# A two-layer attention and retention trunk on one core: another order of work at the opening, between the layers and at the end, and the rotation of the attention's q and k made by VectorE alone

## The chip, the cores and the metric

The kernel runs on one core of one Trainium2 chip. A core has TensorE (PE: matmuls, and transposes made as matmuls), VectorE (DVE), ScalarE (ACT), GpSimd (POOL) and SyncE (SP, which here only issues DMAs). PE writes to PSUM, a memory of eight banks; the other tiles lie in SBUF. The metric is the device time in microseconds (us) of one execution, lower is better. The engines run their own instruction streams and meet only at semaphores, on which an instruction waits until a count is reached.

## The reference, cut to what matters

```python
for layer in range(2):
    h = rms_norm(x, norm_g[layer])                     # x: 1024 rows of 1024
    qa, ka, va, ga, qr, kr, vr, gr, gm = split(h @ w_in[layer])
    qa = rope(rms_norm(qa per head, attn_q_norm))      # 8 heads of 64
    ka = rope(rms_norm(ka per head, attn_k_norm))      # 2 kv heads of 64
    ya = (silu(ga) * softmax(qa ka' / 8) va) @ w_branch_attn[layer]
    yb = (silu(gr) * group_norm(retention(rope(qr), rope(kr), vr))) @ w_branch_ret[layer]
    gates = sigmoid(gm)
    x = x + (gates[0] * ya + gates[1] * yb) @ w_out[layer]
out = rms_norm(x, final_norm_g)

# rope on one head, per axis, with x1, x2 the halves of the axis:
# [x1 * c - x2 * s,  x1 * s + x2 * c]
```

All is float32. A product of float32 matrices is made of three matmuls of two-part numbers (hi and lo, where lo is the number less its rounded hi part): hi·hi, hi·lo and lo·hi. So each operand of a product has a hi tile and a lo tile, which some engine has to make.

## The kernel before, in words

x stays in SBUF (xh, 8 tiles of 128 rows, T = 8). A layer has these stages.

*Projection and preparation for attention, once for each of two groups of heads (j = 0, 1).* For j = 0 a row tile t is normed by VectorE into one of two buffers hb (`norm_x`, L1287; it needs the squares' sums that ScalarE makes at L967, and VectorE's `mean_square`, a chain of twelve tiny instructions), turned by PE (`turn_x`, L591), copied as hi part by ScalarE (`hi_x`, L989), and its lo part made by VectorE (`lo_x`, L1343). Then PE projects q (4 heads), k and v of the tile (`project`, L566 to L568, 24 matmuls of 384 columns). ScalarE squares and copies the result (L1002 to L1004), VectorE sums the squares and frees the bank (`outputs`, L1354, L1357). In three batches VectorE makes the inverse roots (`norms`). Then each tile's q and k, 5 heads of 64 = 320 columns, are normed and rotated (`rotate`, L1380 on): VectorE multiplies by the root and the gain (L1385, L1388) and, with the halves exchanged, by the sines (L1396, two instructions of 160 columns); GpSimd multiplies by the cosines (L420) and adds the two (L425). ScalarE takes the hi parts, VectorE the lo parts (`split`, L1404, L1406), PE turns them (`turn`, L663), and ScalarE and VectorE keep what was turned (L1023, `keep_k` L1412). In the code PE has at the end four gate projections between the turns, each in two parts.

*Attention of the group:* 32 tiles of scores, softmax and values; here PE is kept busy.

*Retention, gates and branches*, which the change does not touch but for the layer number in the semaphores' counts.

*The output product.* The matrix product with w_out is made by a scheme of 7 products of halved matrices (N_P = 7) instead of 8. Product p takes a left operand (a half of xm, or a sum of two, `left_sum`, L1689) and a right one (a block of w_out, or a sum, L537). ScalarE makes their hi parts (L1200, L1218), VectorE the left lo parts (`left_lo`, L1698), GpSimd the right sums and the right lo parts (L544). PE makes product p of 48 matmuls into four banks (L938 to L940), and VectorE adds them to one or two quarters of x (`add_up`, L1711; four banks, one or two instructions of 512 columns each). Two sets of four banks take turns, so product p + 2 waits for `add_up(p)`. A product loops over k outside and the four row tiles i inside, so all four results are complete only at its end.

*Order.* Each engine's order is written out by hand, in the code of its block. The layers are a hardware loop (`Fori(0, DEPTH)`) on every engine, and at the loop's head the engines wait on `phase_end` until PE, ScalarE and VectorE have all drained. At the opening ScalarE issues all constants and waits for them before it issues x; GpSimd makes the hi and lo parts of the first weights (L383, L389); VectorE makes the retention's decay factors (L1298 to L1329) before the loop is entered. At the end of a layer VectorE's order is `add_up(4)`, `add_up(5)`, `mean_square`, two `norm_x`, `add_up(6)`; the last layer's end then norms rows 2 to 7 in place (L1747) and two queues write the rows to `out`.

## Time and profile before

| what | value |
|---|---|
| median of 3 runs | 1934.1 us (1932.88 to 1935.05) |
| the profiled execution's own time | 1931.47 us |
| its span, first to last instruction | 1929.7 us |
| PE busy | 1812.3 us (94%) |
| VectorE busy | 1061.7 us (55%) |
| GpSimd busy | 836.7 us (43%) |
| ScalarE busy | 668.2 us (35%) |
| chain that ended last: PE, VectorE, issue, DMA | 69%, 16%, 6%, 3% |

An engine's busy share is an average over stages with different limits. The chain that ended last is followed back from the last instruction, at each step to what released it. In timelines a row is a start, a duration, the engine, the line, what was written and read, and in brackets how long the engine had been idle before it and who released it. PEclk is the clock granted to TensorE, 1.00 being its full 2.4 GHz and 0.50 the lower level of 1.2 GHz.

### The profile page before, as it was taken

To read this page: it belongs to the slowest core of one execution; us is meant where nothing else is said; L and a number is where in the kernel's file an instruction comes from. 1 tells how busy PE (TensorE), PEld (TensorE's weight loads), DVE (VectorE), ACT (ScalarE), POOL (GpSimd) and SP (SyncE) were. 2 spreads that over 40 slices of the span, in tenths; PEclk is the share of its full clock that TensorE was granted. 3 is DMA by queue.
4 is the path that set the end of the run, shared out by engine and by line. 5 is a ranking of instruction groups with operands and counts; after the bars stand their busy time and mean duration, and the time that the engine had idled before them with its cause. 6 is when DMAs were issued, how large, how long until landed. Compare 5 with 4: busy or idle time off the path is not lost.

```text
span 1929.7 us, 32806 instructions
## 1 busy us (share of the span) xinstructions
PE 1812.3 (94%) x10784; PEld 1590.6 (82%) x10784; DVE 1061.7 (55%) x2246; ACT 668.2 (35%) x1564; POOL 836.7 (43%) x652
## 2 busy tenths in 40 slices
PE   3899989999999999999878998999999999999995
PEld 3788978899999888888667887789999988888874
DVE  6979678635554210107977987794444541110478
ACT  4368438622212100003433872683222210000133
POOL 3348337623422323335823773485223422323383
PEclk9999999999999999999989999999999999999998
DMA  7100000101111111124130001001011111112132
GB/s 248 33 12 13 27 23 23 45 23 44 35 30 34 44 55 44 44 65 164 34 124 23 23 1 49 9 15 45 24 43 43 44 33 44 44 54 65 50 136 88
DMA packets 129593, 96.40 MB, mean 50 GB/s; under 512 B 15664, under 2 KB 114224, under 8 KB 129456
## 3 DMA queue, kind: packets, MB, share of 16 engines
q1 hardware_dynamic: 125920, 84.56, 14.1%
q10 hardware_dynamic: 3536, 10.17, 1.5%
q8 instruction: 66, 1.08, 0.2%
q14 instruction: 71, 0.58, 0.1%
HBM read 82.13 MB, written 12.58 MB: 49 GB/s over the span
## 4 chain that ended last, share of the span: by engine, by line
PE 69%; DVE 16%; issue 6%; DMA 3%; ACT 2%; POOL 2%; DVEq 1%; SPq 1%; ACTq 0%; POOLq 0%
PE ps L566 17%; PE ps L568 17%; PE ps L567 17%; PE ps L701 5%; PE ps L690 4%; DVE xh L1711 3%; PE ps L714 2%; PE ps L716 2%; DMA xh<-xs 2%; PE ps L807 2%; DVE pT_lo L1477 1%; PE ps L791 1%; DVE zqk L1388 1%; DVE rtb L1396 1%; DVE hT_lo L1698 1%
## 5 line engine op out<-in xcount | busy, mean ns | idle before, releaser
L566 PE MATMUL ps<-w_hi,hT_hi 128*128 128x256 f32 (+1 forms) x1280 | 390.3, 305 | 13.9 <-DVE hT_lo L1343 9.3
L568 PE MATMUL ps<-w_hi,hT_lo 128*128 128x256 f32 (+1 forms) x1280 | 376.5, 294 | 0.0
L567 PE MATMUL ps<-w_lo,hT_hi 128*128 128x256 f32 (+1 forms) x1280 | 376.3, 294 | 0.0
L383 POOL TENSOR_SCALAR w_hi<-raw 128x1024 fp32r<-128x1024 f32 x100 | 108.4, 1084 | 398.5 <-PE ps L568 368.4
L566 PEld LDWEIGHTS ps<-w_hi,hT_hi 128*128 128x128 f32 x1280 | 245.0, 191 | 17.4 <-issue 12.5
L566 PE MATMUL ps<-hT_hi,w_hi 128*128 128x512 f32 x640 | 254.6, 398 | 0.0
L567 PE MATMUL ps<-hT_lo,w_hi 128*128 128x512 f32 x640 | 251.1, 392 | 0.0
L568 PE MATMUL ps<-hT_hi,w_lo 128*128 128x512 f32 x640 | 250.8, 392 | 0.0
L567 PEld LDWEIGHTS ps<-w_lo,hT_hi 128*128 128x128 f32 x1280 | 245.2, 192 | 0.3
L568 PEld LDWEIGHTS ps<-w_hi,hT_lo 128*128 128x128 f32 x1280 | 244.6, 191 | 0.0
L389 POOL TENSOR_TENSOR w_lo<-raw,w_hi 128x1024 fp32r<-128x1024 f32 x84 | 207.5, 2470 | 6.0
L435 POOL TENSOR_SCALAR pp<-pp,rrc 128x1024 f32<-128x1024 f32 x128 | 144.4, 1128 | 109.0 <-DVE rrc L1482 102.1
L1667 DVE SCALAR_TENSOR_TENSOR tA<-tA,ps 128x512 f32<-128x512 f32 x32 | 21.8, 686 | 306.9 <-PE ps L568 306.9
L1477 DVE TENSOR_TENSOR pT_lo<-ps,pT_hi 128x512 fp32r<-128x512 f32 x256 | 164.3, 683 | 24.5 <-ACT pT_hi L1072 23.2
L482 POOL TENSOR_TENSOR ra<-ra,rb 128x256 f32<-128x256 f32 x64 | 47.7, 746 | 271.9 <-DVE rb L1532 271.9
L1469 DVE TENSOR_REDUCE nmx<-ps 128x1 f32<-128x1024 f32 x128 | 155.4, 1214 | 2.8 <-PE ps L690 2.8
L701 PE MATMUL ps<-idf,pp 128*128 128x128 f32 x1024 | 146.5, 279 | 10.5 <-DVE pT_lo L1477 8.1
L701 PEld LDWEIGHTS ps<-idf,pp 128*128 128x128 f32 x1024 | 111.2, 140 | 49.6 <-DVE pT_lo L1477 49.0
L1061 ACT ACTIVATE pp<-ps,nmx 128x1024 f32<-128x1024 f32 x128 | 144.2, 1127 | 17.7 <-DVE nmx L1469 16.2
L1072 ACT CAST pT_hi<-ps 128x512 fp32r<-128x512 f32 x256 | 138.5, 590 | 29.6 <-PE ps L701 26.9
L690 PE MATMUL ps<-k_st,q_st 128*128 128x512 f32 x512 | 148.6, 412 | 0.0
L568 PEld LDWEIGHTS ps<-hT_hi,w_lo 128*128 128x128 f32 x640 | 121.4, 190 | 26.0
(175 smaller groups left out, 3543.0 us busy)
## 6 DMA issues: line engine op xcount, KB each, us to landing
raw<-w_in SPq DMA_DIRECT2D x168, 256.0 KB, 3.2
xs<-xh SPq DMA_DIRECT2D x2, 4096.0 KB, 17.6
xh<-xs SPq DMA_DIRECT2D x8, 1024.0 KB, 13.9
xh<-x ACTq DMA_DIRECT2D x4, 1024.0 KB, 10.1
raw<-w_a SPq DMA_DIRECT2D x16, 256.0 KB, 2.9
raw<-w_r SPq DMA_DIRECT2D x16, 256.0 KB, 3.2
w<-w_o SPq DMA_DIRECT2D x4, 1024.0 KB, 11.6
ctA<-rope_a SPq DMA_DIRECT2D x8, 256.0 KB, 2.9
```

Source lines behind the costliest of these rows:

```text
L383: nc.gpsimd.tensor_scalar(place(pos)[0], raw[:, slot], 1.0, 1.0, ALU.mult, ALU.mult).then_inc(w_rounded, 1)
L389: nc.gpsimd.tensor_tensor(lo, raw[:, slot], hi.bitcast(F32), ALU.subtract).then_inc(w_ready, 1)
L435: nc.gpsimd.tensor_scalar(pp[:, tile % 3], pp[:, tile % 3], rrc[:, tile % 4:tile % 4 + 1], 1.0, ALU.mult, ALU.mult).then_inc(p_norm, 1)
L566: nc.tensor.matmul(outp, ah, bh, start=(start and i == 0), stop=False)
L567: nc.tensor.matmul(outp, ah, bl, start=False, stop=False)
L568: last = nc.tensor.matmul(outp, al, bh, start=False, stop=(stop and i == len(pairs) - 1))
L690: last = nc.tensor.matmul(ps[:, 2 * (tile % 2) + n, :], q_st[:, hh, t * P:(t + 1) * P], k_st[:, c, n * 512:(n + 1) * 512], start=(c == 0), ...
L701: last = nc.tensor.transpose(ps[:, 4 + g % 2, kb * P:(kb + 1) * P], pp[:, tile % 3, (4 * half + kb) * P:(4 * half + kb + 1) * P], idf[:])
L1061: nc.scalar.activation(pp[:, tile % 3], ps[:, 2 * s:2 * s + 2].rearrange("p a b -> p (a b)"), ACT.Exp, bias=nmx[:, tile % 4:tile % 4 + 1], ...
L1072: nc.scalar.copy(pT_hi[:, e % 2, 4 * half:4 * half + 4, (tile % 2) * P:(tile % 2 + 1) * P], ps[:, 4 + half].rearrange("p (k c) -> p k c", ...
L1469: V.tensor_reduce(nmx[:, tile % 4:tile % 4 + 1], ps[:, 2 * s:2 * s + 2].rearrange("p a b -> p (a b)"), AXX, ALU.max, negate=True).then_inc ...
L1477: V.tensor_tensor(pT_lo[o], ps[:, 4 + half].rearrange("p (k c) -> p k c", c=P), pT_hi[o].bitcast(F32), ALU.subtract).then_inc(p_lo, 1)
```

## The change

It has three parts.

**The layer loop is written out** on all engines (`for L in range(DEPTH)`), with constant counts in most waits in place of registers, and the wait of all engines for all at the layer's head is gone.

**Opening, border and end have another order.** At the opening SP and ScalarE issue x tile 0 and the first weights at once, the constants behind them. ScalarE makes the first weights' hi parts and VectorE their lo parts. Squares are now taken a row tile at a time (`square_row`, 1024 columns), rows 2 to 7 of them behind `outputs(0)`, `outputs(1)` and `outputs(2)`; VectorE has four `mean_square`s in place of two, and the decay factors stand between its tiles 2 and 6. In the output product, products 3, 4 and 5 change places; the right lo parts go from GpSimd to VectorE, two left sums (for products 5 and 6) from VectorE to GpSimd; product 6 (`last_product`) loops over the row tiles outside, so that they are completed one after another; VectorE's `mean_square` and first norms stand ahead of `add_up(5)`. In layer 0 PE makes the first two `turn_x` of the next layer inside product 6. At the end rows 0 to 3 are normed ahead of `add_up(5)`, rows 4 to 7 in two pairs behind `add_up(6)`.

**VectorE makes the whole rotation** of the attention's q and k: the product with the cosines and the sum, 128x320 each, are its instructions, and GpSimd's two per tile are gone. GpSimd's filling of the gate weights then stands alone ahead of the attention.

```diff
-LEFT = (((1, 0, 1),), ((0, 0, 1), (0, 1, 1)), ((0, 0, 1), (1, 0, -1)), ((1, 0, 1), (1, 1, 1)),
...
-B_SUMMED = (0, 2, 4, 5, 6)
+B_SUMMED = (0, 2, 3, 4, 6)
@@ sync
-            with sp.Fori(0, DEPTH) as L:
+            sp.dma_start(xh[:, 0, 0:512], xt[:, 0, 0:512]).then_inc(x_in[0], 16)
...
+            for L in range(DEPTH):
...
-                            sp.wait_ge(phase_end, 3 + L * PH_L + j * 3)
+                            if j == 0:
+                                sp.wait_ge(o_done, L * (4 * N_P) + 4 * N_P)
+                            else:
+                                sp.wait_ge(phase_end, L * PH_L + j * 3)
@@ gpsimd
                 with pool.Fori(0, KVH) as j:
-                    for t in range(T):
-                        bt = L * (KVH * T) + j * T + t
-                        pool.wait_ge(b_norm, bt * 2 + 2)
-                        if t >= 2:
-                            pool.wait_ge(b_lo, bt * 2 - 2)
-                        nc.gpsimd.tensor_tensor(rta[:, t % 2]..., zqk[:, t]..., ctA[:, 0, t:t + 1]..., ALU.mult).then_inc(b_cos, 1)
-                        pool.wait_ge(b_cos, bt + 1)
-                        pool.wait_ge(b_sin, bt * 2 + 2)
-                        nc.gpsimd.tensor_tensor(rta[:, t % 2], rta[:, t % 2], rtb[:, t % 2], ALU.add).then_inc(b_rot, 1)
-                        if t == 3:
-
-                            pool.wait_ge(b_proj, L * (KVH * T) + j * T + T)
-                            fill(0, 0, L * PER[0] + j * 3 + 2, n0 + j * N_B + 4)
+                    pool.wait_ge(b_proj, L * (KVH * T) + j * T + T)
+                    fill(0, 0, L * PER[0] + j * 3 + 2, n0 + j * N_B + 4)
...
-                right_lo(0)
-                right_lo(1)
                 right_sum(2, 4)
-                right_lo(2)
-                right_lo(3)
-                right_sum(4, 6)
...
+                right_sum(3, 6)
+                right_sum(4, 8)
+                left_sum(5)
                 right_sum(6, 10)
-                right_lo(6)
+                left_sum(6)
@@ tensor
+                def last_product(p):
...
+                    for i in range(4):
+                        pe.wait_ge(o_post, base + POSTS[p - 2] + len(INTO[p - 2]) * (i + 1))
...
+                        if L + 1 < DEPTH and i >= 1 and i <= 2:
+                            pe.wait_ge(o_post, base + POSTS[p - 1] + len(INTO[p - 1]) * (2 * i))
+                            turn_x(i - 1, L + 1)
@@ scalar
+            square_row(0)
+            act.wait_ge(idf_in, 16)
+            nc.scalar.copy(idr[:], idf[:]).then_inc(pro_act, 1)
+            first_hi(0)
+            first_hi(1)
...
                         outputs(t)
+                        if j == 0 and L == 0:
+                            if t < 3:
+                                square_row(2 + 2 * t)
+                                square_row(3 + 2 * t)
@@ vector
+            def mean_square(a, b, squares, nw):
+
+                dve.wait_ge(a_sq, squares)
...
                         if t >= 2:
                             dve.wait_ge(b_rot, bt - 1)
+                            dve.wait_ge(b_lo, bt * 2 - 2)
+                        V.tensor_tensor(rta[:, t % 2].rearrange("p (h d) -> p h d", d=HD), z,
+                                        ctA[:, 0, t:t + 1].to_broadcast([P, GRP + 1, HD]), ALU.mult).then_inc(b_cos, 1)
...
+                        dve.wait_ge(b_cos, bt + 1)
+                        dve.wait_ge(b_sin, bt * 2 + 2)
+                        V.tensor_tensor(rta[:, t % 2], rta[:, t % 2], rtb[:, t % 2], ALU.add).then_inc(b_rot, 1)
...
+                            if L == 0 and t < 2:
+                                if t == 0:
+                                    mean_square(2, 4, 4, 24)
+                                norm_x(0, t + 2)
                             if t == 1:
-                                mean_square(L, 1)
-                            if t + 3 < T:
+                                mean_square(4, 8, SQ0(L + 1) if L == 0 else SQ0(L) + N_SQ, 36 if L == 0 else NW_0 + L * NW_L + 12)
+                            if t + 3 < T and (L or t):
                                 norm_x(L, t + 3)
+                        if j == 0 and L == 0:
+                            if t == 2:
+                                decays_start()
+                            if t == 4:
+                                decays_ratio()
+                            if t == 6:
+                                decays_end()
...
                 add_up(4)
-                add_up(5)
-                mean_square(L + 1, 0)
+
+                mean_square(0, 4, SQ0(L + 1) + 8, NW_0 + (L + 1) * NW_L)
...
+                else:
+                    for t in range(4):
+                        norm_out(t)
+                    add_up(5)
+                    add_up(6)
```

The first place is ScalarE's order at the opening. Before (junk and sqj are where squares go, xh is x, sq and zqk are the squares and the copy of a projected tile):

```order
L960 CAST idr<-idf 128x128
L962 ACTIVATE lgw<-lgw 128x16
L967 ACTIVATE junk,ss<-xh 128x512 x12
L977 ACTIVATE dec<-dec 128x8x6
L982 UNCONDITIONAL_BRANCH
```

And now, from the first copied tile on:

```order
L1023 ACTIVATE junk,ss<-xh 128x1024
L1041 CAST hT_hi<-ps 128x4x128 x2
L1055 ACTIVATE sq<-ps 128x320
L1056 COPY zqk<-ps 128x320
L1057 CAST v_st<-ps 128x64
L1023 ACTIVATE junk,ss<-xh 128x1024 x2
L1041 CAST hT_hi<-ps 128x4x128 x2
L1055 ACTIVATE sq<-ps 128x320
L1056 COPY zqk<-ps 128x320
L1057 CAST v_st<-ps 128x64
L1023 ACTIVATE junk,ss<-xh 128x1024 x2
```

Before, all the squares but four stood ahead of the loop; now each pair of row squares follows the work on a projected tile.

The second place is VectorE, one tile's rotation in the attention's preparation. Before, between the root's product and the next tile's lo part:

```order
L1385 TENSOR_TENSOR zqk<-zqk,rs 128x320
L1387 ISA
L1388 TENSOR_TENSOR zqk<-zqk,gqk 128x320
L1389 REGISTER_ALU
L1396 TENSOR_TENSOR rtb<-zqk,ctA 128x10x16 x2
L1341 REGISTER_ALU
L1343 TENSOR_TENSOR hT_lo<-ps,hT_hi 128x4x128
```

And now:

```order
L1467 TENSOR_TENSOR zqk<-zqk,rs 128x320
L1470 TENSOR_TENSOR zqk<-zqk,gqk 128x320
L1475 TENSOR_TENSOR rta<-zqk,ctA 128x320
L1481 TENSOR_TENSOR rtb<-zqk,ctA 128x10x16 x2
L1485 TENSOR_TENSOR rta<-rta,rtb 128x320
L1424 TENSOR_TENSOR hT_lo<-ps,hT_hi 128x4x128 x2
```

Two instructions of 320 columns have come in on VectorE; there are 8 tiles, 2 groups and 2 layers of them.

The third place is VectorE between the product's additions (xh<-ps,xh) of the first layer, now:

```order
L1811 SCALAR_TENSOR_TENSOR xh<-ps,xh 128x512 x8
L1821 TENSOR_TENSOR ur_hi<-w1x,ur_hi 128x1024 x2
L1798 TENSOR_TENSOR hT_lo<-lsum,hT_hi 128x2x512 x2
L1811 SCALAR_TENSOR_TENSOR xh<-ps,xh 128x512 x8
L1821 TENSOR_TENSOR w_lo<-w1x,w_hi 128x4x256 x2
L1798 TENSOR_TENSOR hT_lo<-xm,hT_hi 128x2x512 x2
L1811 SCALAR_TENSOR_TENSOR xh<-ps,xh 128x512 x4
L1821 TENSOR_TENSOR ur_hi<-w1x,ur_hi 128x1024 x2
L1821 TENSOR_TENSOR w_lo<-raw,w_hi 128x4x256 x2
```

The rows with L1821 are the right lo parts, which were GpSimd's.

## Rows read from the trace of the kernel before

**Rows 1.** Busy time by stretch: two preparations of layer 0, and an attention.
```profile
core 0: us, PE busy (x) PEld busy (x) DVE busy (x) ACT busy (x) POOL busy (x), PEclk, DMA share, GB/s
49.80:98.50 48.70, 41.07 (x232) 36.33 (x230) 45.12 (x109) 16.94 (x48) 18.26 (x18) 0.96 0.08 24
224.70:265.00 40.30, 33.98 (x182) 29.51 (x180) 38.18 (x97) 12.35 (x37) 18.35 (x18) 0.96 0.11 29
113.00:207.00 94.00, 91.37 (x623) 77.96 (x622) 82.58 (x137) 78.62 (x151) 69.59 (x71) 1.00 0.05 13
```
**Rows 2.** Groups by line, 224.7 to 265 us: VectorE's lo parts, GpSimd's rotation.
```profile
L1404 DVE TENSOR_TENSOR qs<-rta,qs 128x256 fp32r<-128x256 f32 x7 | 4.4, 633 | 0.0
L1406 DVE TENSOR_TENSOR qs<-rta,qs 128x128 fp32r<-128x128 f32 x7 | 4.0, 566 | 0.0
...
L420 POOL TENSOR_TENSOR rta<-zqk,ctA 128x320 f32<-128x320 f32 x8 | 7.6, 952 | 28.6 <-DVE zqk L1388 28.6
L425 POOL TENSOR_TENSOR rta<-rta,rtb 128x320 f32<-128x320 f32 x8 | 7.1, 889 | 2.6 <-DVE rtb L1396 2.6
```
**Rows 3.** Timeline of VectorE in the same stretch, single instructions.
```profile
227.86 0.49 DVE L1388 TENSOR_TENSOR zqk<-zqk,gqk 128x320 f32<-128x320 f32 x1
...
245.92 2.57 DVE L1388 TENSOR_TENSOR zqk<-zqk,gqk 128x320 f32<-128x320 f32 x1
...
266.38 0.29 DVE L1406 TENSOR_TENSOR qs<-rta,qs 128x128 fp32r<-128x128 f32 x1
```
**Rows 4.** Timeline of PE at the opening.
```profile
28.21 3.67 PE L591 MATMUL ps<-idf,hb 128*128 128x128 f32 x16 [28.21 <-DVEq L1330]
32.77 0.68 PE L566 MATMUL ps<-w_hi,hT_hi 128*128 128x384 f32 x1 [0.89 <-POOL w_lo L389]
```
**Rows 5.** Timeline of ScalarE: first projection's outputs, and an activation of 1024 columns.
```profile
39.27 0.44 ACT L1002 ACTIVATE sq<-ps 128x320 f32<-128x320 f32 x1 [3.39 <-PE ps L568]
...
107.86 1.11 ACT L1061 ACTIVATE pp<-ps,nmx 128x1024 f32<-128x1024 f32 x1 [1.89 <-DVE nmx L1469]
```
**Rows 6.** Timeline of VectorE: decay factors, a mean square, a norm, batch 0.
```profile
9.39 0.17 DVE L1301 TENSOR_SCALAR lgw<-lgw 128x16 f32<-128x16 f32 x1 [4.30 <-ACT lgw L962]
...
12.40 0.90 DVE L1314 TENSOR_SCALAR dec<-lgw,icol 128x8 f32<-128x8 f32 x6
...
41.97 0.15 DVE L1278 TENSOR_REDUCE ss<-ss 128x4 f32<-128x8 f32 x1
...
44.44 1.29 DVE L1287 SCALAR_TENSOR_TENSOR hb<-xh,rs,gB 128x1024 f32<-128x1024 f32 x1
...
50.43 0.28 DVE L1365 TENSOR_SCALAR gqk<-gqk 128x256 f32<-128x256 f32 x1
```
**Rows 7.** Timeline of PE: a wait of 3 us.
```profile
84.68 0.84 PE L663 MATMUL ps<-idr,qs 128*128 128x128 f32 x6 [3.15 <-DVE qs L1406]
```
**Rows 8.** The stretch behind it, columns as in the first group.
```profile
86.00:88.00 2.00, 2.00 (x6) 1.53 (x5) 1.77 (x7) 0.15 (x1) 0.00 (x0) 0.50 0.53 155
```
**Rows 9.** Timeline of VectorE in the output product of layer 0.
```profile
878.34 2.35 DVE L1698 TENSOR_TENSOR hT_lo<-lsum,hT_hi 128x1024 fp32r<-128x1024 f32 x2
...
940.94 6.76 DVE L1698 TENSOR_TENSOR hT_lo<-lsum,hT_hi 128x1024 fp32r<-128x1024 f32 x2
```
**Rows 10.** Timeline of GpSimd in the same product.
```profile
894.05 4.73 POOL L537 TENSOR_TENSOR w1x<-w1x 128x1024 f32<-128x1024 f32 x2
```
**Rows 11.** Timeline of PE from the last product of layer 0 into layer 1.
```profile
950.06 0.49 PE L938 MATMUL ps<-ur_lo,hT_hi 128*128 128x512 f32 x1 [1.89 <-POOL ur_lo L544]
...
969.43 3.57 PE L591 MATMUL ps<-idf,hb 128*128 128x128 f32 x16 [7.53 <-DVE hb L1287]
...
979.64 0.68 PE L566 MATMUL ps<-w_hi,hT_hi 128*128 128x384 f32 x1 [6.65 <-DVE hT_lo L1343]
```
**Rows 12.** Timeline of VectorE at the end of the kernel.
```profile
1894.85 9.86 DVE L1711 SCALAR_TENSOR_TENSOR xh<-ps,xh 128x512 f32<-128x512 f32 x16
...
1920.78 4.87 DVE L1747 SCALAR_TENSOR_TENSOR xh<-xh,rs,gB 128x1024 f32<-128x1024 f32 x4
```

More of the change, by code:

```diff
@@ L56 @@
 U_L = U_D2
-PH_L = 3 * (KVH + 2)
+PH_L = 3 * (KVH + 1)
 G_BANK = (2, 3, 2, 6)
@@ L154, in build @@
             sqj = sb(pq, "sqj", [512])
+        with ExitStack() as pk:
+            sb(pk, "below_junk2", [2 * SEQ])
+            junk2 = sb(pk, "junk2", [DM])
         with ExitStack() as pb:
@@ L324, in _ @@
                             if j == 0:
+                                for xi in x_in:
+                                    sp.wait_ge(xi, 32 if xi is x_in[0] else 16)
+                                sp.wait_ge(o_post, L * N_POST + N_POST)
                                 sp.dma_start(xs.rearrange("(t p) d -> p t d", p=P), xh[:]).then_inc(x_saved, 16)
                         if j == 0 and i == 0:
-                            sp.wait_ge(consts_in, NCONST)
                             sp.wait_ge(o_blo, L * (2 * N_P) + 2 * N_P)
+                        if L == 0 and j == 0 and i == N_B - 1:
+                            sp.wait_ge(w_ready, 1 + before)
+                            sp.sem_inc(raw_in[0], 32)
                         unit(i % 2, before, parts)
-                with sp.Fori(0, RH) as h:
+                for h in range(0, RH):
                     n0 = u0 + U_C + h * N_C
@@ L334, in _ @@
                         unit(i % 2, n0 + (i - 1 if i else 0), cols(i % 2, L, c0 + h * RD))
-                with sp.Fori(0, K // 2) as mm:
+                for mm in range(0, K // 2):
                     n0 = u0 + U_D1 + mm * (2 * N_D1)
@@ L368, in _ @@
                 x_block(1, 0)
-            for t in range(1, T, 2):
-                put_out(sp, t)
-            sp.wait_ge(out_done[1], 16 * (T // 2))
+            for t in range(T):
+                if t not in OUT_ACT:
+                    put_out(sp, t)
+            sp.wait_ge(out_done[0], 16 * (T - len(OUT_ACT)))
         @block.gpsimd
@@ L578, in w_u, with turn_x @@
                 return w_hi[:, k, a:b], w_lo[:, k, a:b]
-            pe.wait_ge(consts_in, NCONST)
+            pe.wait_ge(idf_in, 16)
             pe.wait_ge(pro_act, 1)
             pe.sem_inc(o_done, 4 * N_P)
-            pe.drain().then_inc(phase_end, 1)
-            with pe.Fori(0, DEPTH) as L:
-                def turn_x(t):
+            for L in range(DEPTH):
+                def turn_x(t, L=L):
                     pe.wait_ge(h_ready, L * T + t + 1)
@@ L1311, in _ @@
-            half = DEPTH * RH
-            for c in range(6):
-                a = (c % 2) * half
-                ins = V.tensor_scalar(dec[:, :, c], lgw[:, 2, a:a + half], icol[:, c:c + 1], None, ALU.mult)
-                if c == 5:
-                    step(ins)
-                else:
-                    ins.then_inc(pro_dve, 1)
-                    done[0] += 1
-            assert done[0] == 22, done
-            mean_square(0, 0)
-            dve.wait_ge(gain_in, 16)
-            norm_x(0, 0)
@@ L1332, in _, with lo_x @@
                 dve.sem_inc(s, 1)
-            dve.drain().then_inc(phase_end, 1)
-            with dve.Fori(0, DEPTH) as L:
-                dve.wait_ge(phase_end, 3 + L * PH_L)
-                def lo_x(t):
+            V.memset(ss4[:, T:], 0.0).then_inc(a_zero, 1)
+            dve.wait_ge(a_zero, 1)
+            mean_square(0, 1, 1, 0)
+            dve.wait_ge(gain_in, 16)
+            norm_x(0, 0)
+            first_lo(0)
+            first_lo(1)
+            for L in range(DEPTH):
+                def lo_x(t, L=L):
                     for hf in range(2):
@@ L1714, in _, with right_lo @@
                     merge(b)
+                def right_lo(p):
+                    if p == 0:
+                        dve.wait_ge(o_blo, L * (2 * N_P) + 2 * N_P)
+                    for h in range(2):
+                        dve.wait_ge(o_bhi, L * (2 * N_P) + 2 * p + h + 1)
+                        hi, lo = right_slot(p, h)
+                        V.tensor_tensor(lo, right_src(p, h), hi.bitcast(F32), ALU.subtract).then_inc(o_blo, 1)
                 left_sum(2)
```

339 lines of the change are left out of this document (203 added, 136 removed).

## Prediction

> **What bounds the kernel now.** I read the table of busy shares and the chain that ended last first: PE is busy for 94% of the span and holds 69% of the chain, VectorE 16%. An average says little, so the busy time by stretch comes next [rows 1]. In the attention PE is busy 91.37 of 94 us; nothing that the change touches can be felt there. In the preparations it is the other way round: in 48.7 us VectorE is busy 45.12, in 40.3 us 38.18, and PE waits for it. The two of layer 1 are within 0.4 us of these. So there are four stretches, some 178 us together, in which each microsecond that VectorE gets more of makes the kernel longer. Last I read the timelines at the opening, at the border of the layers and at the end, where PE stands still: 28.21 us ahead of its first work [rows 4], 7.53 + 6.65 us at the border [rows 11], and everything behind the last product at the end [rows 12].
>
> **Term A, the rotation.** Per stretch 8 tiles get two more VectorE instructions of 320 columns. The same shape takes 0.49 us, with a pitch near 0.52 [rows 3]: 16 x 0.52 = +8.3 us a stretch, +33 in all. What comes back is the time in which GpSimd's 16 instructions (0.95 and 0.89 us each, 14.7 us a stretch [rows 2]) slowed VectorE. The lo part of 128 columns takes 0.29 us alone and 0.57 in the mean of this stretch, that of 256 columns 0.63 and some 0.35 alone: 7 x (0.28 + 0.28) = 3.9 us for j = 1 [rows 2, 3]. For j = 0 I put 3.0, since its tiles have more work between the rotations. The one large pause, 2.57 against 0.49 us [rows 3], belongs to the filling of the gate weights, which stays. Small idle times of VectorE (1 to 2 us a stretch) take up a little: +5.1, +4.4, +4.6 and +4.4, so **+18.5**. Bounds: 4 x (8.3 - 3.9 - 2.1) = +9, if the idle time takes up all it can, and +33, if nothing comes back. Nothing else waits longer for it: GpSimd's fill waits only for the last projection.
>
> The Trainium skill ("SBUF — State Buffer", section "SBUF: two separate sides") says that VectorE and GpSimd share a port pair under an exclusive lock, held for the whole instruction. That speaks against my 3 to 3.9 us: by it all 14.7 us of a stretch could come back, and the term would be 4 x (8.3 - 14.7) = -26 us. Only the fill's pause of 2.57 looks like it in this trace; the lo parts lose 0.28 us, not 0.9.
>
> **Term B, the opening.** x tile 0 no longer waits behind the constants, the mean square is of one row, the first weights are made by two engines, and the decay factors (9.39 to 13.30 [rows 6]) are out of the way. I let the first projection start about 11.5 us earlier than 32.77 [rows 4], at 21.3; 9 to 13 are possible. But then come two chains that did not exist, since all squares were then taken ahead. Rows 2 and 3 are squared by ScalarE only behind `outputs(0)`. From 21.3: projection until its outputs 6.5 (32.77 to 39.27 [rows 4, 5]), outputs 1.0, two squares of 1.3 (1.11 for 1024 columns [rows 5] and the sum's reading) 2.6, mean square 2.4 (41.97 to 44.44), norm 1.2 [rows 6]: 35.0. Then the turn 0.9, and `project(1)` starts near 36, where PE has stood some 7 us. A wait of 3.15 us is followed by a stretch granted 0.50 of the clock, the level of 1.2 GHz [rows 7, 8], so this one costs up to 1.5 us more. `project(1)` ends at 41.4, turn and `project(2)` at 46.4, outputs 47.4, squares 6 and 7 50.0, mean square 52.4, `norm_x(4)` 53.6. Before it ended at 45.65 [rows 6]. From there VectorE needs 3.8 us more (sums, a lo part, a norm) until batch 0: 57.4 instead of 50.43 [rows 6], **+7.0**.
>
> From batch 0 on VectorE is the bound, so whatever is put in counts whole: the decay factors, 21 tiny instructions and more, 0.4 + 3.9 (9.39 to 13.30) + 0.4 = +4.7; minus the 1.2 us of idle time that the old start of the stretch had. The opening without rotation: 7.0 + 4.7 - 1.2 = **+10.5**. Bounds: -8, if the 11.5 us carried through and only the decay factors were paid (-11.5 + 3.5); +14, if the low clock comes twice and for long.
>
> **Term C, the output product of layer 0 and the border.** Seven right lo parts go to VectorE, 2.35 us each alone [rows 9], +16.5 us; it loses two left sums (4.6 as contended). GpSimd, which took about 5 us for a lo part, ends its chain earlier, so the last product no longer waits 1.89 us for it [rows 11]. The question is how the pairs of 128x1024 instructions fall: 2.35 alone, 6.76 while GpSimd runs its own [rows 9]; GpSimd's 4.73 [rows 10] likewise stretch. Setting out the order by hand with every second pair stretched, the products start 2 to 4 us later (the last at 953.9 instead of 950.06), `add_up(4)` ends at 956.6 (952.5 before: half of the 9.86 from 947.6). Then the gain: mean square and first norms stand ahead of `add_up(5)`, and PE turns the first tiles inside the product. Before, norms began 13.5 us behind `add_up(4)`; now the mean square waits only for four squares, 3.1 us. First turn 966.9, first projection of layer 1 near 976 instead of 979.64 [rows 11]: -3.6. With no pause at all the same order gives 963.8: -16. I take **-7**, nearer to the slow end, because both engines have 128x1024 work almost all through this stage. VectorE's rows completed one by one cost PE nothing: 48 matmuls as before (950.06 to 961.90, PE's start at 969.43 less its 7.53 idle [rows 11]).
>
> **Term D, the product of layer 1 and the end.** The same delay of products (+2 to +4), no border behind it. After `add_up(4)` the chain was 4.9 + 3.1 + 2.4 + 2 norms + `add_up(6)` + two `norm_out` + mean square + four `norm_out`: from 1899.8 to 1925.65 [rows 12], 25.9 us. Now it is squares 3.1, mean square 2.4, four norms 4.9, `add_up(5)` 4.9, `add_up(6)` 2.4, squares and mean square 4.8, four norms 4.9 [rows 12], = 27.4; the output's DMA behind it, some 4 us, remains. So +1.5 for the chain, +2.5 for the products; but the left sums and the stall for the right lo part that went give back some 3: **+1**. Bounds -6 (no pauses) and +5.
>
> **Nothing for the loop written out.** The wait for all at the layer's head goes, but PE waits for VectorE's norm there in any case. Registers turned to constants are the sequencers' work, which runs ahead. Bounds -2 to 0.
>
> **Sum.** 18.5 + 10.5 - 7 + 1 = +23 us on the profiled execution's 1931.5 = 1954.5; the median of the runs lies 2.6 above the profiled one, so 1957.
>
> **The rivals.**
> 1. The pauses between the two engines vanish in the output products, because VectorE's lo parts fall where GpSimd waits. For it: GpSimd is idle for 30 us more there. Against it: every sum of GpSimd now has a lo part of VectorE to run against. C -16 and D -6 instead of -7 and +1: 1957 - 16 = 1941.
> 2. The opening's head start carries through: ScalarE finds time for the squares while PE projects, or VectorE has slack behind them. For it: ScalarE is busy a third of the time. Against it: in its order the squares stand behind `outputs(0)`, which waits for the projection. B = -8: 1957 - 18.5 = 1938.5. With rival 1 together 1922, faster.
> 3. The low clock comes oftener: the preparations have more PE idle time (9 to 13 us each instead of 7), and each stretch like [rows 8] costs 2 to 3 us where PE is then needed at once. Three more in the opening and one in each stretch: +12, 1969. Against it: PE is not the bound there.
> 4. The other side, faster: VectorE and GpSimd exclude each other whole, in the preparations. Place: `rotate`; price: all 14.7 us of a stretch [rows 2] come back against 8.3. It decides once more than 8.3 us a stretch come back. Then A is -26 and the whole 18.5 + 26 less: 1957 - 44 = 1913. Against it: VectorE was busy for 38.18 of 40.3 us [rows 1], and its instructions that overlap GpSimd's show 3 to 4 us of excess, no more.
>
> **How the numbers follow.** Forecast 61%, with a range of its own of 1949 to 1965. Rival 1 14%, rival 2 7%, the two together 3%, rival 3 10%, rival 4 5%. The range reaches from rival 2 to rival 3: 1938 to 1969. Less than 0.2% (3.9 us) is about what a measurement can't tell from no change. Faster needs a time below 1930: rival 4 and both of 1 and 2 together, 8%. Within 0.2%: 1930 to 1938, the low tails of rivals 1 and 2, 6%. Slower: 86%.
>
> **What would show it.** Right if the profile after has the first projection near 21 us, two idle times of PE of some 7 us at the opening, VectorE's batch 0 near 57, each preparation of j = 1 longer by 4 to 5 us with VectorE busy for nearly all of it, the lo parts of 128 columns at 0.29 us, and the first projection of layer 1 3 to 7 us closer to the end of the preparations than before. Wrong if batch 0 stands at 50 or earlier, if a preparation is no longer than before, or if the products start earlier than before against their stage's begin.

## The result, and the profile after

The changed kernel takes 1946.1 us (median of 4, 1944.18 to 1947.58), the kernel before 1934.57 (4 runs). The ratio is 1.0060, 95% interval 1.0043 to 1.0078: slower by 11.5 us. That lies in the range given, but it is half of what was forecast, and three of the four terms of the sum came out far from their forecasts, in both directions.

First, VectorE's timeline of the changed kernel at the opening and at the end (start, duration, engine, line, what was written and read, idle time and releaser), which answers to [rows 6, 12]:

```profile
29.81 0.16 DVE L1343 TENSOR_REDUCE ss<-ss 128x2 f32<-128x4 f32 x1 [7.19 <-ACT junk L1023]
...
49.06 0.16 DVE L1343 TENSOR_REDUCE ss<-ss 128x4 f32<-128x8 f32 x1 [10.44 <-ACT junk L1023]
...
56.50 0.28 DVE L1447 TENSOR_SCALAR gqk<-gqk 128x256 f32<-128x256 f32 x1
...
1907.78 4.87 DVE L1811 SCALAR_TENSOR_TENSOR xh<-ps,xh 128x512 f32<-128x512 f32 x8
1915.70 0.16 DVE L1343 TENSOR_REDUCE ss<-ss 128x4 f32<-128x8 f32 x1 [3.06 <-ACT junk L1015]
...
1918.09 4.87 DVE L1356 SCALAR_TENSOR_TENSOR xh<-xh,rs,gB 128x1024 f32<-128x1024 f32 x4
1922.87 7.39 DVE L1811 SCALAR_TENSOR_TENSOR xh<-ps,xh 128x512 f32<-128x512 f32 x12
1932.71 0.16 DVE L1343 TENSOR_REDUCE ss<-ss 128x2 f32<-128x4 f32 x1 [2.45 <-ACT junk L1015]
...
1939.83 2.48 DVE L1356 SCALAR_TENSOR_TENSOR xh<-xh,rs,gB 128x1024 f32<-128x1024 f32 x2
```

VectorE twice waits for ScalarE's squares at the opening, 7.2 and 10.4 us, and batch 0 begins at 56.50. At the end, add_up(4) ends at 1912.65 and the last norm at 1942.3: 29.7 us, where it was 25.9.

The groups by line of the second preparation of layer 0 in the changed kernel (busy, mean ns of one, idle before), which answer to [rows 2]:

```profile
L1481 DVE TENSOR_TENSOR rtb<-zqk,ctA 128x160 f32<-128x160 f32 x16 | 4.4, 318 | 0.0
L1485 DVE TENSOR_TENSOR rta<-rta,rtb 128x320 f32<-128x320 f32 x8 | 3.9, 492 | 1.2 <-DVE rtb L1481 0.5
L1475 DVE TENSOR_TENSOR rta<-zqk,ctA 128x320 f32<-128x320 f32 x8 | 3.9, 492 | 0.3
L1492 DVE TENSOR_TENSOR qs<-rta,qs 128x256 fp32r<-128x256 f32 x8 | 3.3, 417 | 0.0
...
L1494 DVE TENSOR_TENSOR qs<-rta,qs 128x128 fp32r<-128x128 f32 x8 | 2.3, 285 | 0.0
```

And the row of the same view for the sine products in the kernel before:

```profile
L1396 DVE TENSOR_TENSOR rtb<-zqk,ctA 128x160 f32<-128x160 f32 x16 | 9.9, 660 | 0.3
```

This is the row that I had not weighed. The products with the sines took 660 ns each in the mean, now 318, and I had taken the mean for their price. It is the mean of two kinds. The view of one line gives shortest, median and longest in ns; here are the sine products and the lo parts of 128 columns, both before:

```profile
L1396 DVE TENSOR_TENSOR rtb<-zqk,ctA x16: 324/654/1005, 228.4 to 262.7; 128x160 f32<-128x160 f32 x16
L1406 DVE TENSOR_TENSOR qs<-rta,qs x8: 278/284/964, 234.0 to 266.4; 128x128 fp32r<-128x128 f32 x8
```

And one tile's pair of sine products as single instructions, with GpSimd's cosine product:

```profile
228.38 0.32 DVE L1396 TENSOR_TENSOR rtb<-zqk,ctA 128x160 f32<-128x160 f32 x1
228.43 1.01 POOL L420 TENSOR_TENSOR rta<-zqk,ctA 128x320 f32<-128x320 f32 x1 [13.55 <-DVE zqk L1388]
228.63 0.99 DVE L1396 TENSOR_TENSOR rtb<-zqk,ctA 128x160 f32<-128x160 f32 x1
```

The first began ahead of GpSimd's instruction and took 0.32 us. The second began inside it, took 0.99, and ended 0.18 us after it. It is so in all 32 pairs of the kernel before: 0.32 or 0.33 us, then 0.98 to 1.01, with the end always 0.18 or 0.19 us behind GpSimd's. So the unslowed price did stand in the trace before, in every other instruction.

The busy times from batch 0 to the last lo part of each preparation; the kernel before, busy times by stretch:

```profile
224.74:266.67 41.93, 35.60 (x193) 30.95 (x192) 39.70 (x101) 13.73 (x40) 18.35 (x18) 0.96 0.10 28
996.70:1046.41 49.71, 41.80 (x238) 37.02 (x237) 46.05 (x112) 17.71 (x48) 18.26 (x18) 0.97 0.07 22
```

and the changed kernel:

```profile
56.50:112.84 56.34, 44.22 (x236) 39.73 (x236) 48.76 (x152) 16.91 (x48) 3.55 (x2) 0.89 0.07 19
237.07:278.18 41.11, 35.54 (x194) 31.04 (x193) 37.38 (x117) 13.56 (x40) 3.55 (x2) 0.96 0.10 29
1007.13:1057.01 49.88, 43.52 (x240) 38.54 (x239) 44.76 (x128) 17.48 (x48) 3.55 (x2) 0.93 0.18 62
```

VectorE has 16 instructions more in a preparation (101 to 117, the third count of a row) and is busy 2.3 us less (39.70 to 37.38). The three stretches of the changed kernel that got only the rotation are 0.8 us shorter, 0.2 longer and 0.8 longer than before.

PE's waits in the changed kernel, which answer to [rows 11]: at product 2 of layers 0 and 1, and inside the last product of layer 0.

```profile
915.69 0.76 PE L970 MATMUL ps<-ur_hi,hT_hi 128*128 128x512 f32 x1 [2.85 <-issue]
...
981.82 1.97 PE L624 MATMUL ps<-idf,hb 128*128 128x128 f32 x8 [13.71 <-DVE xh L1811]
...
1863.31 0.47 PE L970 MATMUL ps<-ur_hi,hT_hi 128*128 128x512 f32 x1 [4.29 <-issue]
```

The span of the profiled executions, 1929.7 and 1945.5, splits at the same points of both kernels like this (the forecasts are the prediction's terms):

| stretch | before | after | difference | forecast |
|---|---|---|---|---|
| start to batch 0, layer 0 | 50.4 | 56.5 | +6.1 | +7.0 |
| batch 0 to the preparation's last lo part | 49.7 | 56.3 | +6.6 | +8.6 |
| to the last lo part of j = 1 | 166.5 | 165.3 | -1.2 | +4.4 |
| to the start of the output product | 602.7 | 601.7 | -1.0 | 0 |
| product and border, to batch 0 of layer 1 | 127.3 | 127.2 | -0.1 | -7 |
| to the last lo part of its preparation j = 1 | 217.1 | 217.0 | 0 | +9.0 |
| to the start of the output product | 602.7 | 601.9 | -0.8 | 0 |
| product and end | 113.2 | 119.4 | +6.2 | +1 |

The output product is taken to start with VectorE's first left sum. The differences add to +15.8. The medians say 11.5; the profiled execution of before lies 3 us under its median, and that of after 1.5 over.

### The profile page after: what moved, and what is told of

It reads as the page before. It is cut to its first block, busy times and chain, and to the rows that moved or that the text cites. A ratio compares the mean times of both kernels' runs of the same rounds, so it can differ in the third digit from the quotient of the medians.

```text
span 1945.5 us, 30041 instructions
## 1 busy us (share of the span) xinstructions
PE 1815.9 (93%) x10784; PEld 1601.5 (82%) x10784; DVE 1062.5 (55%) x2370; ACT 666.0 (34%) x1551; POOL 708.5 (36%) x562
## 4 chain that ended last, share of the span: by engine, by line
PE 73%; DVE 14%; issue 4%; POOL 4%; ACT 3%; DMA 1%; POOLq 0%; SPq 0%; ACTq 0%; DVEq 0%
PE ps L600 17%; PE ps L602 17%; PE ps L601 17%; PE ps L733 4%; PE ps L722 3%; PE ps L746 2%; PE ps L748 2%; DVE pT_lo L1579 2%; PE ps L839 2%; DVE xh L1811 1%; POOL pp L470 1%; PE ps L823 1%; PE ps L970 1%; PE ps L972 1%; PE ps L971 1%
## 5 line engine op out<-in xcount | busy, mean ns | idle before, releaser
L429 POOL TENSOR_SCALAR w_hi<-raw 128x1024 fp32r<-128x1024 f32 x97 | 103.1, 1062 | 583.7 <-PE ps L602 543.8
L600 PEld LDWEIGHTS ps<-w_hi,hT_hi 128*128 128x128 f32 x1280 | 246.7, 193 | 10.8 <-DVE v_st L1439 4.9
L435 POOL TENSOR_TENSOR w_lo<-raw,w_hi 128x1024 fp32r<-128x1024 f32 x81 | 199.6, 2464 | 5.8
L733 PE MATMUL ps<-idf,pp 128*128 128x128 f32 x1024 | 140.7, 278 | 15.7 <-DVE pT_lo L1579 9.1
## 6 DMA issues: line engine op xcount, KB each, us to landing
xh<-x SPq DMA_DIRECT2D x2, 1024.0 KB, 10.4
```

Of the source, the lines that this page charges most:

```text
L429: nc.gpsimd.tensor_scalar(place(pos)[0], raw[:, slot], 1.0, 1.0, ALU.mult, ALU.mult).then_inc(w_rounded, 1)
L435: nc.gpsimd.tensor_tensor(lo, raw[:, slot], hi.bitcast(F32), ALU.subtract).then_inc(w_ready, 1)
L600: nc.tensor.matmul(outp, ah, bh, start=(start and i == 0), stop=False)
L733: last = nc.tensor.transpose(ps[:, 4 + g % 2, kb * P:(kb + 1) * P], pp[:, tile % 3, (4 * half + kb) * P:(4 * half + kb + 1) * P], idf[:])
```

## The experiments

All ratios are against the kernel before, run on the same chip.

**The rotation alone.** The kernel before, with the two instructions of rotate(t) taken over by VectorE (GpSimd's filling of the gate weights then stands alone, as in the changed kernel; the code is shortened):

```diff
 vector, rotate(t)
+    V.tensor_tensor(rta[:, t % 2]..., z, ctA[:, 0, t:t + 1]..., ALU.mult).then_inc(b_cos, 1)
     for s in range(2): ...                    # the sine products
+    V.tensor_tensor(rta[:, t % 2], rta[:, t % 2], rtb[:, t % 2], ALU.add).then_inc(b_rot, 1)
 gpsimd
-    nc.gpsimd.tensor_tensor(rta..., zqk..., ctA..., ALU.mult).then_inc(b_cos, 1)
-    nc.gpsimd.tensor_tensor(rta..., rta..., rtb..., ALU.add).then_inc(b_rot, 1)
```

> The kernel before with the third part of the change alone: VectorE makes the cosine product and the sum, GpSimd none of them; opening, border and end as before. Theory 1 (what is read from the two traces now): the two products with the sines, 1.23 us before and 0.56 us after, had never run alone before, so that 8 x 0.67 = 5.4 us a stretch come back beside the 3 to 4 us at the lo parts, against 8.3 us added: each stretch changes by -1 to +1 us, and the whole kernel by less than 4 us (0.2%), ratio 0.998 to 1.002. Theory 2 (the prediction's term A): only 3 to 3.9 us a stretch come back, each stretch is 4.4 to 5.1 us longer, +18.5 us, ratio 1.0096.

Measured: 1931.55 us, ratio 0.9986 (0.9977 to 0.9995). The stretches are 50.3, 41.5, 50.3 and 41.6 us, before 49.7, 41.9, 49.7 and 41.9. Theory 1 holds, and the prediction's term A falls: the rotation on VectorE costs nothing. (That the sine products had never run alone before is not so: the first of each pair did, as shown above.)

**The rotation given back.** The reverse edit, in the changed kernel.

> The changed kernel with the cosine product and the sum given back to GpSimd (two instructions a tile, the gate weights' filling behind tile 3 as before); opening, border and end as changed. Theory 1: the same 1946 us within 4 us, the sine products back at 1.2 us, the lo parts partly at 0.9. Theory 2: 18.5 us less, near 1928. What is left over the kernel before (+12) is then the price of the new orders alone.

Measured: 1947.22 us, ratio 1.0068 (1.0055 to 1.0082). The two agree: the rotation's part of the change is worth -1 to -3 us (the -1, from 1947.22 against 1946.10, is within the intervals of the two ratios), and the new orders alone cost 13 us.

**One of the two instructions at a time.** In cos_only VectorE makes the cosine product and GpSimd the sum, in sum_only the reverse; everything else is the kernel before.

> The kernel before with only the cosine product moved to VectorE; GpSimd keeps the sum. It tells which of GpSimd's two instructions holds which of VectorE's. If the cosine product is what ran beside the sine products, these fall to 0.56 us here and the pause of about 0.65 us goes on with the sum: at the lo parts or what else follows. Theory 1: 8 x 0.52 = 4.2 us added and 8 x 0.67 = 5.4 us back a stretch, so -1 us a stretch, -4 us in all; if the sum now holds another instruction for 0.5 us that it did not before, 0. Theory 2: +4.2 us a stretch, +17 us.

> The kernel before with only the rotation's sum moved to VectorE; GpSimd keeps the cosine product. The counterpart of cos_only. Theory 1 (the cosine product on GpSimd is what held the sine products): these stay at 1.2 us here, while the lo parts fall to 0.42 and 0.28 us; 4.2 us a stretch added and 3 to 4 us back, so each stretch changes by 0 to +1.5 us; the kernel comes to 1934 to 1941, 10 us or more over cos_only, though as many instructions have moved. Theory 2 (the gain of cos_only is not the sine products', but chance or the order of the rest): the sine products change here as well, and the time is within 3 us of cos_only's 1923.6.

Measured: cos_only 1923.59 us, ratio 0.9948 (0.9932 to 0.9963); sum_only 1936.75, ratio 1.0021 (1.0012 to 1.0031). The groups by line of the second preparation, cos_only:

```profile
L1401 DVE TENSOR_TENSOR qs<-rta,qs 128x256 fp32r<-128x256 f32 x8 | 4.6, 578 | 0.0
L1393 DVE TENSOR_TENSOR rtb<-zqk,ctA 128x160 f32<-128x160 f32 x16 | 4.4, 318 | 0.0
L1403 DVE TENSOR_TENSOR qs<-rta,qs 128x128 fp32r<-128x128 f32 x8 | 4.3, 532 | 0.0
```

and sum_only:

```profile
L1393 DVE TENSOR_TENSOR rtb<-zqk,ctA 128x160 f32<-128x160 f32 x16 | 9.9, 660 | 0.3
L420 POOL TENSOR_TENSOR rta<-zqk,ctA 128x320 f32<-128x320 f32 x8 | 7.6, 950 | 36.6 <-DVE zqk L1385 36.6
L1382 DVE TENSOR_TENSOR zqk<-zqk,rs 128x320 f32<-128x320 f32 x8 | 5.6, 702 | 0.1
...
L1404 DVE TENSOR_TENSOR qs<-rta,qs 128x256 fp32r<-128x256 f32 x7 | 2.9, 418 | 0.0
```

GpSimd's cosine product held the second sine product of each pair (660 instead of 318 ns in the mean, with 16 of them 5.5 us a stretch). Its sum held mostly lo parts (578 and 532 instead of 417 and 285 ns in the mean, 3.3 us a stretch). Against 4.2 us for each of the two on VectorE, the cosine product pays (5.5 back) and the sum doesn't (3.3 back). The best division is the one that neither kernel has.

The lengths of the stretches bear the signs out: cos_only has 48.4, 40.8, 48.4 and 40.8 us, 5.0 less than before in all, and sum_only 51.9, 43.3, 51.8 and 42.8, 6.6 more. Its two stretches of j = 0 are 2.1 us longer, beyond the 0 to +1.5 expected; why is open. In its second stretch the filling of the gate weights, and not the sum, held a root product and a lo part of 128 columns (702 ns is the root products' mean, 0.48 us their usual time), so not all of these lo parts fell to 0.28 us. Not all of cos_only's gain comes from its stretches either. Its profiled execution is 8.2 us shorter than that of before, and 2.0 of that is the first projection, which took 4.46 us until ScalarE's first squares where before took 6.50; in 4 us PE made 24 matmuls there instead of 13. rot_alone's did the same, sum_only's didn't. Whether that belongs to the kernels or to the single executions profiled is not shown.

**The squares earlier.** In the changed kernel ScalarE squares rows 2 to 5 behind row 1, rows 6 and 7 behind hi_x(1):

```diff
-                            square_row(1)
+                            for r in range(1, 6):
+                                square_row(r)
...
+                        if j == 0 and t == 0 and L == 0:
+                            square_row(6)
+                            square_row(7)
...
-                            if t < 3:
-                                square_row(2 + 2 * t)
-                                square_row(3 + 2 * t)
```

> The changed kernel, with ScalarE squaring rows 2 to 5 right behind row 1 and rows 6 and 7 behind the second tile's hi parts, all ahead of outputs(0), in place of a pair behind each of the first three outputs. Theory A (the prediction's term B): the two chains through the squares cost the opening its head start; batch 0 of VectorE starts near 40 us in place of 56.5, PE's idle times of 7 us ahead of the turns of tiles 2 and 4 go, and since VectorE is the bound from there on most of it, 12 to 16 us, comes out at the end: 1930 to 1934. Rival: x, the tables and the weights arrive too late for that or PE's projections become the bound (5.05 us each), so that batch 0 starts early but the stretch behind it is longer; under 6 us gained, 1940 or more.

Measured: 1935.82 us, ratio 1.0010 (1.0001 to 1.0019), so 10 us under the changed kernel, less than the 12 to 16 expected. Batch 0 begins at 44.32 instead of 56.50, and the stretch behind it is as long as in the changed kernel (56.2 us): theory A holds in kind. Two waits stand between 44.3 and the 40 expected. The squares of row 4 waited for x, and PE still stood 3.9 us ahead of the turn of tile 2:

```profile
20.71 1.06 ACT L1023 ACTIVATE junk<-xh 128x1024 f32<-128x1024 f32 x1 [2.74 <-DMA xh<-x]
```

```profile
31.31 1.16 PE L624 MATMUL ps<-idf,hb 128*128 128x128 f32 x8 [3.92 <-DVE hb L1353]
```

The second wait has little to do with the squares. The norm was late because the mean square ahead of it took 5.1 us instead of 2.4, beside GpSimd's filling of the next weights:

```profile
26.79 2.34 POOL L435 TENSOR_TENSOR w_lo<-raw,w_hi 128x1024 fp32r<-128x1024 f32 x1
...
26.94 2.21 DVE L1334 TENSOR_TENSOR nt<-nt,ss 128x2 f32<-128x2 f32 x1
```

An instruction on two columns, 0.16 us elsewhere, lasted until GpSimd's had ended.

**The decay factors in the gaps.**

```diff
                                 if t == 0:
+                                    decays_start()
+                                    decays_ratio()
                                     mean_square(2, 4, 4, 24)
                                 norm_x(0, t + 2)
+                                if t == 1:
+                                    decays_end()
...
-                            if t == 2:
-                                decays_start()
-                            if t == 4:
-                                decays_ratio()
-                            if t == 6:
-                                decays_end()
```

> The changed kernel with the decay factors made in VectorE's idle times of the opening: start and ratio ahead of the mean square of rows 2 and 3 (VectorE stands 7.2 us there), the end behind the norm of tile 3 (10.4 us there), in place of between the tiles behind batch 0. Theory A (term B: what is put into the stretch in which VectorE is the bound counts whole): the last split of the stretch comes 4.9 to 5.3 us earlier (4.5 + 0.8 us of instructions), batch 0 itself stays at 56 to 57, the kernel gains about 5 us: 1941. Rival: the stretch has slack for them, its last split moves by less than 1.5 us, and so does the kernel.

Measured: 1941.26 us, ratio 1.0032 (1.0021 to 1.0043), 5 us under the changed kernel. ScalarE's two exponentials for the factors move with them. Batch 0 is at 58.2, 1.7 us later than it was (56 to 57 expected), the last lo part at 108.1 instead of 112.8, 4.7 us earlier. The stretch between them is 49.9 us instead of 56.3, nearly as long as that of before, so little else had lengthened it. Theory A holds.

**add_up(5) right behind add_up(4), and one mean square at the end.**

```diff
                 add_up(4)
+                add_up(5)
                 mean_square(0, 4, SQ0(L + 1) + 8, NW_0 + (L + 1) * NW_L)
...
                     norm_x(L + 1, 1)
-                    add_up(5)
...
                         norm_out(t)
-                    add_up(5)
                     add_up(6)
-            for t in (4, 6):
-                mean_square(t, t + 2, SQ0(DEPTH) + 12 + t - 2, nw)
-                nw += 12
-                for i in range(2):
-                    norm_out(t + i)
+            mean_square(4, 8, SQ0(DEPTH) + N_SQ, nw)
+            for t in range(4, 8):
+                norm_out(t)
```

> The changed kernel with add_up(5) right behind add_up(4) in both layers, where VectorE waits some 3 us for squares anyway, and one mean square of rows 4 to 7 at the end in place of two of a pair each. Theory B (the new order of the additions is what lost the gain at the border and lengthened the end): in layer 0 PE no longer stands 13.7 us inside the last product for the banks of product 5, the first projection of layer 1 comes 2 to 3 us earlier; at the end 3.1 us of waiting and one mean square of 2.4 us go and the squares of add_up(5) are out of the way, 5 to 7 us. Together 7 to 10 us: 1936 to 1939. Rival: the last product or the output's DMA ends last anyway, less than 3 us.

Measured: 1935.78 us, ratio 1.0006 (0.9998 to 1.0015), 10 us under the changed kernel. From the start of the output product to the first projection of layer 1 it takes 109.4 us instead of 111.7; product and end of layer 1 take 111.5 instead of 119.4. The size that theory B gives is right at both places, but not its account of the border. PE still stands there, 12.1 us instead of 13.7, and is now released by the norm:

```profile
979.64 1.94 PE L624 MATMUL ps<-idf,hb 128*128 128x128 f32 x8 [12.11 <-DVE hb L1352]
```

Which of its two edits gave what at the end was not measured apart.

**right_lo(2) ahead of add_up(0).**

```diff
-                add_up(0)
                 right_lo(2)
+                add_up(0)
```

> The changed kernel with right_lo(2) ahead of add_up(0) on VectorE. In the changed kernel add_up(0) waits 6.1 and 7.5 us for x to come back from memory, and right_lo(2), which product 2 needs, stands behind it; PE then stands 2.9 us (layer 0) and 4.3 us (layer 1) ahead of product 2. Theory C (the work moved from GpSimd to VectorE was queued behind a wait): both go, the products from 2 on start 3 to 4 us earlier and the kernel gains 5 to 7 us: 1939 to 1941. Rival: the operands of the later products are late in any case, since VectorE has more to do there; the time is given back at product 5 or 6, and less than 2 us are gained.

Measured: 1938.47 us, ratio 1.0020 (1.0011 to 1.0028), 7.6 us under the changed kernel. add_up(4) ends at 961.75 instead of 965.03 in layer 0. In the changed kernel VectorE's order and waits were

```profile
909.58 4.88 DVE L1811 SCALAR_TENSOR_TENSOR xh<-ps,xh 128x512 f32<-128x512 f32 x8 [6.08 <-DMA xh<-xs]
914.37 2.35 DVE L1821 TENSOR_TENSOR ur_hi<-w1x,ur_hi 128x1024 fp32r<-128x1024 f32 x2
```

and with the edit

```profile
907.22 3.58 DVE L1821 TENSOR_TENSOR ur_hi<-w1x,ur_hi 128x1024 fp32r<-128x1024 f32 x2 [4.07 <-ACT ur_hi L1288]
910.72 4.87 DVE L1811 SCALAR_TENSOR_TENSOR xh<-ps,xh 128x512 f32<-128x512 f32 x8
```

Product 2 of layer 0 now waits 0.2 us instead of 2.9. Theory C holds: the lo part that product 2 needs stood behind a wait for x from memory; put ahead of it, it is made 7 us earlier (it now waits for ScalarE's hi part), and add_up(0) finds x there.

**All together.** best_a has the edits of the last two experiments, the rotation of cos_only, and a further order of the opening: the squares of rows 2 and 3 stand behind row 1 and those of rows 4 to 7 behind hi_x(1), decays_start() and the mean square of rows 2 and 3 behind norm_x(0, 1), decays_ratio() behind norm_x(0, 2), decays_end() behind norm_x(0, 3), and the last constant is issued ahead of x tiles 4 to 7. best_b is the same with the rotation all on VectorE:

```diff
                     lo_x(0)
                     first_lo(2)
                     mean_square(1, 2, 2, 12)
                     norm_x(0, 1)
+                    decays_start()
+                    mean_square(2, 4, 4, 24)
...
                                 norm_x(0, t + 2)
+                                if t == 0:
+                                    decays_ratio()
```

> All of it together: the changed kernel with squares 2 and 3 ahead of the second tile's hi parts and 4 to 7 behind them, the decay factors in idle times of the opening, right_lo(2) ahead of add_up(0), add_up(5) behind add_up(4), one mean square at the end, and the rotation's sum back on GpSimd while VectorE keeps the cosine product. If the theories hold and the stages add: 10 to 14 (opening) + 5 (decay factors) + 7 to 10 (additions) + 5 to 7 (right_lo(2)) + 4 to 8 (the sum on GpSimd, as in cos_only against rot_alone) = 31 to 44 us under the changed kernel: 1902 to 1915, faster than both. If gains of the opening and of the decay factors overlap: up to 1922.

> The kernel of best_a with the rotation's sum on VectorE as in the changed kernel, so both instructions of the rotation there. Theory 1: against best_a (1906.1) it is slower by what rot_alone is against cos_only (1931.6 against 1923.6, 8 us; by the lengths of the four stretches 5 us): 1911 to 1914. Rival: with the other orders VectorE has slack in the preparations, and the two are within 2 us.

Measured: best_a 1906.07 us, ratio 0.9851 (0.9837 to 0.9865), faster than both kernels; best_b 1910.37, ratio 0.9884 (0.9868 to 0.9901). As differences from the kernel before, the four edits took 9.7, 5.4, 10.4 and 7.7 us from the changed kernel's +11.6, 33.2 in all; best_b stands at -22.4, which is 34.0 less. So they add, though best_b's opening is not exactly that of the two experiments on it. The sum on GpSimd is worth 4.3 us more by the medians of best_a and best_b, a little less than the 5 to 8 expected, 6.4 by their ratios, and 5.9 by the lengths of the four stretches; the rival, within 2 us, falls. Batch 0 of best_a begins at 43.2 us, its preparations take 47.9, 40.4, 47.9 and 40.4, and PE's wait ahead of product 2 is gone:

```profile
891.02 0.50 PE L977 MATMUL ps<-ur_hi,hT_hi 128*128 128x512 f32 x1 [0.17 <-DVE xh L1813]
...
954.86 1.94 PE L631 MATMUL ps<-idf,hb 128*128 128x128 f32 x8 [12.19 <-DVE hb L1360]
```

The 12.2 us at the border of the layers remain. The changed kernel's trace shows what fills the wait there:

```profile
968.08 0.16 DVE L1343 TENSOR_REDUCE ss<-ss 128x4 f32<-128x8 f32 x1 [3.05 <-ACT junk L1015]
...
969.58 2.34 POOL L435 TENSOR_TENSOR w_lo<-raw,w_hi 128x1024 fp32r<-128x1024 f32 x1
969.76 2.19 DVE L1333 TENSOR_TENSOR nt<-nt,ss 128x4 f32<-128x4 f32 x1
...
974.14 5.24 DVE L1352 SCALAR_TENSOR_TENSOR hb<-xh,rs,gB 128x1024 f32<-128x1024 f32 x2
```

VectorE waits 3.05 us for squares. Then, beside GpSimd's filling of the next layer's weights, the mean square takes 6.0 us instead of 2.4, and the two norms 5.24 instead of 2.48. The kernel before has the same there (5.3 and 5.27 us). No run here has another order of that filling, so what it would give back is not shown.

## Why the prediction came out as it did

**Term A, +18.5 forecast, -1 to -3 measured: the step that failed.** It is "what comes back is the time in which GpSimd's 16 instructions slowed VectorE", put at 3 to 3.9 us a stretch. I took that time from the means of the lo parts alone, and took the mean of the sine products, 660 ns, for their price. Counted by single instructions, the trace before has in the second preparation eight sine products held for 0.67 us each, 5.4 us, and lo parts and one root product held for 4.0 us, 9.4 in all; in the first it is 8.4. Against 8.3 us added that gives about 0, as measured. There were two hints in the trace before: 324 ns as the shortest of the sine products, and 160 columns taking 0.66 us in the mean where 320 columns of the same operation took 0.49.

Rival 4 had the right mechanism and the wrong amount. It did exclude whole: in the four preparations every slowed VectorE instruction ends a fixed time behind GpSimd's, 0.15 us with 128 columns, 0.18 or 0.19 with 160, 0.28 with 256 and 0.33 to 0.35 with 320. The "0.28 us, not 0.9" at which the prediction dismissed this was again a mean: of eight lo parts of 128 columns five took 0.28 or 0.29 us and three 0.94 to 0.96. But GpSimd's time comes back only where such an instruction stands in wait. During the rest of the 14.7 us VectorE ran what is not held: the sine product already begun, `outputs` (0.47 and 0.21 us beside the sum), the copy of the turned k.

The Trainium skill ("SBUF — State Buffer", section "SBUF: two separate sides") has the two engines share a port pair under an exclusive lock: of a VectorE instruction with two inputs in SBUF and a GpSimd instruction that reads SBUF, the one that starts first has it whole and the other blocks. The trace agrees. In the preparations all the held instructions read two tiles in SBUF, and the sums of squares, which read one, took 0.47 us beside GpSimd's sum as elsewhere. By that section the 14.7 us of the prediction are only an upper bound, for VectorE instructions with one such input are left out; the runs gave 8.4 to 9.4.

**Term B, +10.5 forecast (7.0 and 3.5), +6.1 and about +6 measured** (6.6 less the 0.5 by which rot_alone lengthened this stretch; rot_back, without the rotation, has 5.9; the 1.2 us of idle time taken off for the start of the stretch did not come). Right step by step but for that: the first projection at 20.3 (21.3 forecast), PE idle 7 us ahead of the turns of tiles 2 and 4, batch 0 at 56.5 (57.4). squares_early and decays_gap show both causes. Rival 2, the head start that carries through, did not happen since the squares stood where the order said.

**Term C, -7 forecast, 0 measured.** Two steps failed. The products were to come 2 to 4 us later because of stretched pairs. add_up(4) ends 85.1 us behind the stage's start instead of 83.1, so the size is right, but in lo2_early, where PE's wait of 2.9 us ahead of product 2 is gone, it ends at 82.2: the stretched pairs (4.5 us for 2.35) did not make the products late, and the delay was the lo part queued behind add_up(0). I had written what the moved instruction costs, and not what it is queued behind. And "PE turns the first tiles inside the product" did not shorten the border: PE stood 13.7 us with half of the last product still to do. The first norm, which the turn reads, was written only at 977.4, 12.4 us behind add_up(4), for the reasons shown under best_a. The other 4.4 us are the banks: the turns go into those of product 5, which add_up(5), now behind the norms, frees only near 982.

**Term D, +1 forecast, +6.2 measured.** The products came 3.3 us later (2.5 forecast), by the same wait ahead of product 2, 4.3 us here, and the 3 us that were to be given back by work that left did not show. The chain behind add_up(4) took 29.7 us instead of 27.4: the squares of add_up(5), which now stand behind the norms, hold those of rows 4 to 7 (the mean square waited 2.45 us), and the last rows have a mean square of their own, which the term had left out.

By the profiled executions the forecast was 7 us too high (+23 against +15.8): some 19 too much for A, 12 too little for C and D. By the medians it was 11 too high. That the range held the time is owed in part to luck: two misses point in opposite directions. One of the prediction's own signs of being wrong came true, a preparation no longer than before, and the sign for term C, a first projection of layer 1 3 to 7 us closer, did not: it comes 713.4 us behind the end of the layer's last preparation, before 713.0. Rival 1, no pauses in the product, is not what was seen; rival 3, the low clock, shows in the first stretch (granted 0.89, where [rows 1] has 0.96), but there VectorE is the bound.

## What to carry to other kernels

A mean can hide two kinds. Before calling the mean time of an instruction its price, look at its shortest and longest, and compare its time per column with its neighbours'; here every other sine product took half the mean. When two engines slow each other, find which instruction is held by which, and try each division of the work, since the best may be the one in between. When work is moved to another engine, look at what stands ahead of it in that engine's order, above all an instruction that waits for a transfer. When an order frees a buffer later, look for who was to write into it in the meantime.

## What the runs showed of the hardware that was not expected

A VectorE product of 128x160 took 0.32 us, or 0.98 to 1.01 when it began inside a GpSimd product of 128x320 (950 ns), with its end 0.18 or 0.19 us behind the other's. A VectorE instruction on 4 columns, 0.16 us elsewhere, took 2.19 beside a GpSimd instruction of 1024 columns. VectorE's sums of squares (0.47 us) were not held beside GpSimd's sum. Moving the right one of two equal instructions took 10.8 us off 1934 by the medians (5.0 of it in the four preparations), moving both 2.9, and moving the wrong one cost 4.
